# Query and key tiles woven between the SSM heads and the end of the convolution, and gates through tanh, in a two-layer hybrid encoder

## What is computed

```
xn  = RMSNorm(h)
u   = xn @ W_in
br  = [attention(u), conformer(u), ssd(u), fourier(u)]
h  += W_o( sum_b sigmoid(xn @ Wg_b + c_b) * br_b )
h  += FFN(RMSNorm(h))      # dense in layer 0, 8 experts top-2 in layer 1
h  += sigmoid(h @ Wpg) * (p[l] @ Wpp)
```

## Time and profile before

| | |
|---|---|
| median of 3 runs | 2463.49 us |
| lowest, highest | 2458.93, 2463.57 us |
| the profiled execution: time, span | 2454.93 us, 2453.2 us |
| mean granted clock of TensorE | 0.96 of full speed |
| PE busy, share of the span | 93% |
| DVE, ACT, POOL busy | 65%, 53%, 4% |
| layer 0 mixers, from the start to the norm ahead of the feed-forward | about 0 to 545 us |
| layer 1 mixers | about 787 to 1322 us |

### The profile page before, as it was taken

How to read it: one execution, slowest core, us unless ns; L and a number is a source line. 1 busy time by engine, 2 the same in 40 slices (tenths; PEclk the granted TensorE clock), 3 DMA queues, 4 the chain that set the end, 5 groups by cost and what they waited for, 6 DMA issues and landing times.

```text
span 2453.2 us, 38341 instructions
## 1 busy us (share of the span) xinstructions
PE 2290.8 (93%) x12832; PEld 2000.1 (82%) x12832; DVE 1601.3 (65%) x2481; ACT 1297.4 (53%) x1710; POOL 103.5 (4%) x120
## 2 busy tenths in 40 slices
PE   7979999979997997999997999999999999999997
PEld 6959788979996986878897787878787878788786
DVE  4974233655542795333454898989898989888882
ACT  4421345444432531145543776767676767777671
POOL 0041010000000022011000000000000000000000
PEclk9979999999999998999998999999999999999999
DMA  6413232525533431323332897979898989888881
GB/s 248 173 52 133 99 125 99 196 108 206 177 146 133 168 138 55 142 99 121 139 118 104 337 367 306 371 298 366 309 369 324 365 315 359 336 332 342 332 318 68
DMA packets 76073, 539.40 MB, mean 220 GB/s; under 512 B 8607, under 2 KB 8607, under 8 KB 11976
## 3 DMA queue, kind: packets, MB, share of 16 engines
q1 hardware_dynamic: 72188, 525.03, 56.5%
q0 software_dynamic: 3584, 12.58, 1.8%
q10 hardware_dynamic: 204, 0.54, 0.1%
HBM read 537.03 MB, written 1.10 MB: 219 GB/s over the span
## 4 chain that ended last, share of the span: by engine, by line
PE 84%; DVE 7%; issue 5%; ACT 3%; DMA 1%; DVEq 0%; ACTq 0%; SPq 0%
PE ps L491 22%; PE ps L742 19%; PE ps L744 18%; PE ps L743 18%; PE ps L686 2%; DVE cvfa L1440 2%; DVE wlo L1714 1%; PE ps L892 1%; PE ps L920 1%; ACT whi L1247 1%; PE ps L636 1%; PE ps L696 1%; PE ps L497 1%; DVE xn L1395 0%; DVE ring_lo L1403 0%
## 5 line engine op out<-in xcount | busy, mean ns | idle before, releaser
L1714 DVE TENSOR_TENSOR wlo<-ring,whi 128x1024 fp32r<-128x1024 f32 x746 | 874.5, 1222 | 149.3 <-ACT whi L1247 148.2
L1247 ACT ACTIVATE whi<-ring 128x1024 fp32r<-128x1024 f32 x746 | 749.4, 1054 | 117.8 <-PE ps L744 109.8
L744 PE MATMUL ps<-whi,xlo 128*128 128x512 f32 (+1 forms) x1160 | 428.7, 370 | 0.0
L742 PE MATMUL ps<-whi,xhi 128*128 128x512 f32 x904 | 374.9, 415 | 1.3 <-DVE wlo L1714 1.3
L743 PE MATMUL ps<-wlo,xhi 128*128 128x512 f32 x904 | 355.5, 393 | 0.0
L743 PE MATMUL ps<-xlo,whi 128*128 128x256 f32 x1024 | 292.5, 286 | 0.0
L491 PE MATMUL ps<-xn,ring 128*128 128x256 f32 x1280 | 286.9, 382 | 0.0
L491 PEld LDWEIGHTS ps<-xn,ring 128*128 128x128 f32 x1280 | 245.6, 193 | 33.9
L744 PEld LDWEIGHTS ps<-whi,xlo 128*128 128x128 f32 x1160 | 219.8, 190 | 39.0
L742 PE MATMUL ps<-xhi,whi 128*128 128x256 f32 x736 | 213.6, 290 | 24.0 <-DVE wlo L1714 9.8
L742 PE MATMUL ps<-whi,hhi 128*128 128x512 f32 (+1 forms) x576 | 213.4, 370 | 0.0
(11 more groups left out here) (237 smaller groups left out, 3421.9 us busy)
## 6 DMA issues: line engine op xcount, KB each, us to landing
ring<-w_experts SPq DMA_DIRECT2D x340, 1024.0 KB, 5.0
ring<-w_mixers SPq DMA_DIRECT2D x114, 1024.0 KB, 4.8
ring<-w_dense SPq DMA_DIRECT2D x33, 1024.0 KB, 4.8
ring<-w_ple SPq DMA_DIRECT2D x10, 1024.0 KB, 4.9
bias<-bias_rows POOLq DMA_DIRECT2D x16, 384.0 KB, 4.3
cvfa<-bias_rows POOLq DMA_DIRECT2D x16, 384.0 KB, 4.3
constants_sb<-constants SPq DMA_DIRECT2D x1, 1048.0 KB, 7.9
h<-x_in SPq DMA_DIRECT2D x1, 1024.0 KB, 5.5
```

What stands on the lines that cost most here:

```text
L742: pe.matmul(dst, lhs[0], rhs[0], start=first, stop=False, skip_group_check=True)
L744: return pe.matmul(dst, lhs[1], rhs[0], start=False, stop=last, skip_group_check=True)
L1247: act.activation(whi[:, slot, :], ring[:, j % RING, lo:lo + UNIT], ACT.Copy).then_inc(s_wh, 1)
L1714: dve.tensor_tensor(wlo[:, slot, :], ring[:, j % RING, lo:lo + UNIT], whi[:, slot, :], ALU.subtract).then_inc(s_wl, 1)
```

## The change

- TensorE: `conv_norm` and the old `ssm_heads` leave their places. After `ssm_prep`, `query_key_heads` runs the first heads' cumulative sums, and then, four times: five query or key tiles, the outputs of the two heads, the cumulative sums of the next two. The two sums of the LayerNorm come behind the third tile of the third and of the fourth step, into bank 3. Four tiles are left for the end. Loops are written out.
- VectorE: the last 28 convolution operations go into the first two head steps, 14 each, behind the mixing matrices; the centring goes into the third step and the scaling into the fourth. The zeroing of `mix` moves ahead of the convolution's part that stays. `head_y` waits for both heads' outputs, which share bank 2.
- ScalarE: exponentials, tile copies, root and SiLU in the matching order; the root for the SSM norm behind tile 20.
- `ssm_out`'s transposes go to banks 0 and 1 and no longer wait for the last tile copies; `attention` no longer waits at its start for ScalarE's copies of the SSM branch, but at its first transposes. GpSimd lays out pair i once tile 20 + i is copied and the last mixing matrix is made.
- Gates: sigmoid(x) is taken as (tanh(x/2) + 1)/2. ScalarE computes Tanh with scale 0.5 and half the bias (`half_b`, one small VectorE operation for each layer), VectorE adds 1 in the multiplication, and the factor 0.5 goes into `mix_out` and `ple`.

```diff
+CONV_LATE = CT * CONV_K - 28
...
-            def query_key(l, i, t):
+            def query_key(l, t):
...
+                if t < 2:
+                    pe.wait_ge(s_xtc, l * TT + (t + 1))
+                elif t < 4:
+                    pe.wait_ge(s_sc, l * 2 + (t - 1))
+                else:
+                    pe.wait_ge(s_pf, l * N_PROJ + (T_Q + t - 3))
...
-                chain(bank(7, second * SEQ, SEQ), [con("ones")] * CT, [cv[:, t, :] for t in range(CT)]).then_inc(s_lns, 1)
+                chain(bank(3, 0, SEQ), [con("ones")] * CT, [cv[:, t, :] for t in range(CT)]).then_inc(s_lns, 1)
...
+            def head_y(l, hh):
+
+                for g in range(SSM_GROUPS):
+                    pe.wait_ge(s_mm, l * SSM_HEADS + (2 * hh + g + 1))
...
+            def query_key_heads(l):
+
+                cumsums(l, 0)
+                for hh in range(SSM_HEADS // SSM_GROUPS):
+                    for t in range(5):
+                        query_key(l, 5 * hh + t)
+                        if hh >= 2 and t == 2:
+                            conv_norm(l, hh - 2)
+                    head_y(l, hh)
+                    if hh < SSM_HEADS // SSM_GROUPS - 1:
+                        cumsums(l, hh + 1)
+                for t in range(20, 24):
+                    query_key(l, t)
...
             def ssm_out(l):
                 pe.wait_ge(s_yc, l * SSM_YC + SSM_YC)
-                pe.wait_ge(s_pf, l * N_PROJ + N_PROJ)
...
+                    if u == 0:
+                        pe.wait_ge(s_ybs, l + 1)
...
-                    pe.wait_ge(s_ybs, l + 1)
+                    pe.wait_ge(s_pf, l * N_PROJ + N_PROJ)
...
-                conv_norm(l, 0)
-                conv_norm(l, 1)
                 ssm_prep(l)
-                ssm_heads(l)
+                query_key_heads(l)
                 ssm_out(l)
...
+                for hh in range(SSM_HEADS // SSM_GROUPS):
+                    decay(l, hh, 0)
+                    query_key(l, 5 * hh)
+                    decay(l, hh, 1)
+                    for t in range(1, 4):
+                        query_key(l, 5 * hh + t)
+                    if hh == 3:
+                        conv_root(l)
+                    query_key(l, 5 * hh + 4)
+                conv_silu(l)
+                query_key(l, 20)
                 act.wait_ge(s_yc, l * SSM_YC + 4)
                 act.activation(yst[:, 4:6], yst[:, 2:4], ACT.Sqrt).then_inc(s_ya, 1)
+                for t in range(21, 24):
+                    query_key(l, t)
...
-                act.activation(gs[:, m_ % 2, :], bank(first_bank + m_ % banks, SEQ, SEQ), ACT.Sigmoid,
-                               bias=pk[:, bass.ds(b * KT + (AT["b_gate"] + m_), 1)]).then_inc(s_sg, 1)
+                act.activation(gs[:, m_ % 2, :], bank(first_bank + m_ % banks, SEQ, SEQ), ACT.Tanh,
+                               bias=half_b[:, bass.ds(b * KT + m_, 1)], scale=0.5).then_inc(s_sg, 1)
...
                     head_mix(l, hh, n, 1)
+                    if hh < 2:
+                        conv(l, CONV_LATE + 14 * hh, CONV_LATE + 14 * hh + 14)
+                    elif hh == 2:
+                        conv_center(l)
+                    else:
+                        conv_scale(l)
                     for g in range(SSM_GROUPS):
                         head_y(l, hh, n, g)
...
-                dve.wait_ge(s_y, n + (g + 1))
+                dve.wait_ge(s_y, n + 2)
...
-                dve.tensor_tensor(gt[:, m_ % 2, :], gs[:, m_ % 2, :], bank(first_bank + m_ % banks, 0, SEQ), ALU.mult).then_inc(s_bt, 1)
+                dve.scalar_tensor_tensor(out=gt[:, m_ % 2, :], in0=gs[:, m_ % 2, :], scalar=1.0,
+                                         in1=bank(first_bank + m_ % banks, 0, SEQ), op0=ALU.add,
+                                         op1=ALU.mult).then_inc(s_bt, 1)
...
-                dve.memset(mix[:, :, :], 0.0).then_inc(s_mz, 1)
...
-                    dve.tensor_tensor(h[:, m_, :], h[:, m_, :], bank(m_ % 4, 0, SEQ), ALU.add).then_inc(s_hr, 1)
+                    dve.scalar_tensor_tensor(out=h[:, m_, :], in0=bank(m_ % 4, 0, SEQ), scalar=0.5, in1=h[:, m_, :],
+                                             op0=ALU.mult, op1=ALU.add).then_inc(s_hr, 1)
...
+                dve.tensor_scalar(half_b[:, :], par("b_gate", 0, N_BRANCHES * KT), 0.5, None, ALU.mult)
...
-                conv(l, 8 * EARLY_BLOCKS - 88, CT * CONV_K)
-                conv_norm(l)
+                dve.memset(mix[:, :, :], 0.0).then_inc(s_mz, 1)
+                conv(l, 8 * EARLY_BLOCKS - 88, CONV_LATE)
                 ssm_scores(l)
...
-                    pool.wait_ge(s_pf, l * N_PROJ + N_PROJ)
+                    pool.wait_ge(s_pf, l * N_PROJ + i + (T_Q + 21))
                     n = l * UNITS + i * 4
                     pool.wait_ge(s_s, n + 1)
-                    pool.wait_ge(s_yc, l * SSM_YC + 1)
+                    pool.wait_ge(s_mm, l * SSM_HEADS + SSM_HEADS)
```

More of the change, by code:

```diff
@@ L163, in trunk_program @@
         rms_t = sb("rms_t", [P, 2, SEQ])
+        half_b = sb("half_b_gate", [P, N_BRANCHES * KT])
         mixers = ExitStack()
@@ L622, in ssm_prep @@
                     m.then_inc(s_bc, 1)
[L624 to L647, removed]
@@ new lines, in cumsums @@
+            def cumsums(l, hh):
+                for g in range(SSM_GROUPS):
+                    pe.wait_ge(s_ua, l * SSM_HEADS + (2 * hh + g + 1))
+                    for part in range(4):
+                        m = pe.matmul(bank(g, part * P, P), con("ones"), ua[:, g, part, :], start=True, stop=True)
+                    m.then_inc(s_r, 1)
+            def head_y(l, hh):
+                for g in range(SSM_GROUPS):
+                    pe.wait_ge(s_mm, l * SSM_HEADS + (2 * hh + g + 1))
+                    for tt, parts in enumerate((((0, 0), (3, 0), (4, 1)), ((1, 0), (2, 1), (5, 1)))):
+                        lo = hh * 64 + g * 256
+                        m = chain(bank(2, g * P + tt * 64, 64), [mm_[:, g, b, :] for b, _ in parts],
+                                  [xs[:, s, lo:lo + 64] for _, s in parts])
+                    m.then_inc(s_y, 1)
@@ L1120, in ssm_heads @@
                     act.activation(xs[:, tt, :], bank(4 + tt), ACT.Copy).then_inc(s_xtc, 1)
[L1121 to L1136, removed]
+                for hh in range(SSM_HEADS // SSM_GROUPS):
[9 more added lines that the diff above has]
+                query_key(l, 20)
                 act.wait_ge(s_yc, l * SSM_YC + 4)
                 act.activation(yst[:, 4:6], yst[:, 2:4], ACT.Sqrt).then_inc(s_ya, 1)
+                for t in range(21, 24):
+                    query_key(l, t)
                 act.wait_ge(s_yt, l + 1)
                 for c in range(CT):
-                    m = act.activation(ybr[:, SSM * CT + c, :], bank(4 + c // 2, (c % 2) * SEQ, SEQ), ACT.Copy,
+                    m = act.activation(ybr[:, SSM * CT + c, :], bank(c // 2, (c % 2) * SEQ, SEQ), ACT.Copy,
                                        scale=par("ssm_norm", c))
@@ L1347, in ple @@
                         act.wait_ge(s_pt, l * KT + (m_ - 1))
-                    act.activation(gs[:, m_ % 2, :], bank(2 * (m_ % 2) + 1, 0, SEQ), ACT.Sigmoid).then_inc(s_pg, 1)
+                    act.activation(gs[:, m_ % 2, :], bank(2 * (m_ % 2) + 1, 0, SEQ), ACT.Tanh,
+                                   scale=0.5).then_inc(s_pg, 1)
             act.dma_start(relb_sb, relb).then_inc(s_relL, 16)
@@ L1533, in ssm_heads @@
             def ssm_heads(l):
-                with dve.Fori(0, SSM_HEADS // SSM_GROUPS) as hh:
-                    dve.wait_ge(s_sc, l * 2 + 2)
-                    dve.wait_ge(s_xtc, l * TT + TT)
+                dve.wait_ge(s_sc, l * 2 + 2)
+                dve.wait_ge(s_xtc, l * TT + TT)
+                for hh in range(SSM_HEADS // SSM_GROUPS):
                     n = l * SSM_HEADS + hh * 2
@@ L1875, in ple @@
                     dve.wait_ge(s_pg, l * KT + (m_ + 1))
-                    dve.tensor_tensor(mix[:, m_, :], gs[:, m_ % 2, :], bank(2 * (m_ % 2), 0, SEQ),
-                                      ALU.mult).then_inc(s_pt, 1)
+                    dve.scalar_tensor_tensor(out=mix[:, m_, :], in0=gs[:, m_ % 2, :], scalar=1.0,
+                                             in1=bank(2 * (m_ % 2), 0, SEQ), op0=ALU.add, op1=ALU.mult).then_inc(s_pt, 1)
                 dve.wait_ge(s_pt, l * KT + KT)
                 for m_ in range(KT):
-                    dve.tensor_tensor(h[:, m_, :], h[:, m_, :], mix[:, m_, :], ALU.add).then_inc(s_hr, 1)
+                    dve.scalar_tensor_tensor(out=h[:, m_, :], in0=mix[:, m_, :], scalar=0.5, in1=h[:, m_, :],
+                                             op0=ALU.mult, op1=ALU.add).then_inc(s_hr, 1)
             dve.sem_inc(s_bm, 2)
```

40 lines of the change are left out of this document (22 added, 18 removed).

## The result

The changed kernel takes 2379.04 us (median of 4 runs, 2371.9 to 2381.32) against 2461.21 for the kernel before (4 runs, 2457.08 to 2463.57): a ratio of 0.9663, 95% interval 0.9637 to 0.9689, so 82 us less, by the interval 77 to 89. Of the profiled executions the one after has a span of 2377.2 us against 2453.2, 76.0 less. Forecast were 76 us, and 2387 with a range from 2369 to 2407.

The account below looks back on a forecast made before the run. TensorE, holding 84% of the chain, was taken as the bound. Per layer 32.4 (reordering) + 5.8 (Tanh) - 0.2 (small edits) = 38.0 us saved, 76 in all: 2387 us against the median, range 2369 to 2407.

Parts of the forecast that it names:

- First term: From the end of TensorE's transposes to the query stage: a wait of 4.3 us a layer, ends 3.2 and 6.7.
- the two readings of the lock: GpSimd's `ua` held for VectorE's whole run of taps (4.3 us, chosen), or slipping in between two taps (3.2).
- Second term: Query stage: tiles, cumulative sums, head outputs and LayerNorm sums without gaps on TensorE, 102.5 us a layer.
- The cover: TensorE's work in each head step hides the other engines' chain; with fourteen taps VectorE is free 4.6 us early.
- Third term: Tail from the last query tile through transposes to the second scores: 8.0 us a layer, without a wait.
- The half clock behind the wait for `ua`: TensorE slowed after standing still about 1 us before `ua`: 1.5 us a layer charged, ends 0 and 3.0.
- Fourth term: Attention's gates: Tanh needs no table load beside Exp, saving 5.8 us a layer, ends 0 and 8.8.
- the loads stay: Rival at attention's gates: table loads remain with Tanh, so nothing is saved there; 2399 us, 8%.
- the stage runs at the lower clock: Rival in the query stage: clock stays at 0.50, tiles cost 83 us more a layer; 90 slower, 2553; 2%.
- the head chain outlasts its cover: Rival in the query stage: VectorE becomes the bound in a step, costing 16.7 us a layer; 2421 us, 9%.

Follow-up runs that it names:

- the second profile: Profile of the changed kernel run again, unedited: 2376.80 us, ratio 0.9661 to the kernel before.
- the taps ahead: The changed kernel with all 124 convolution operations ahead of the group scores again, none between the heads: 2400.44 us, ratio 0.9749 to the kernel before.

## Why the prediction was right, and where it was off

**First term, the wait ahead of the query stage: right.** Forecast were taps to 140.3 on the old scale and `ua` 2.76 behind. In the profile after the last tap ends at 145.76, `ua` at 148.52, again 2.76 behind. Tiles start at 149.56, 4.1 after the transposes against 4.3 (5.0 in the second profile, where the wait for `ua` was 1.8 us instead of 0.9). The choice between the two readings of the lock, which decided that term, is what the taps ahead show: one GpSimd operation held for the whole run of taps, and 12.56 us of TensorE's time with it. The Trainium skill (SBUF — State Buffer, Who interferes with whom) says that a VectorE instruction with two SBUF inputs contends with a GpSimd instruction that reads SBUF; that the pair is held "for the whole instruction" stands there beside VectorE's two-port modes, and I had read it for both. By a hold of one instruction that wait would not have been there. Both readings occur, though: where GpSimd's first operation came in the middle of a run of taps it was held to the run's end, in the kernel before, in the changed one and with the taps ahead; where it came two VectorE operations ahead of the taps, at 104.61, GpSimd took turns with them. What decides between the two no run here shows, so the forecast's choice was right for its place and no rule.

**Second term, the query stage: right.** 149.56 to 251.98 are 102.4 us against 102.5. The cover was even longer than computed: in step two VectorE stood idle for 6.6 us before its head outputs, not 4.6, since its chain to the mixing matrices took 9.6 us instead of 11.5; in the order before, each of ScalarE's exponentials stood behind a tile copy (copies at 193.92 and 197.36, exponentials at 194.20 and 197.64). In step four the scaled output came at 237.60, 22.95 behind the step's sums at 214.65 (forecast 22.9), against the outputs' end at 238.11. That 0.5 us of room held.

**Third term, the tail: right.** 251.98 to 259.81 are 7.8 us against 8.0.

**The half clock behind the wait for `ua`: oversized.** I charged 1.5 a layer. Neither profile of the changed kernel had half clock between transposes and second scores, with waits of 0.9 and of 1.8 us; behind the 12.56 us hole it came.

**Fourth term, Tanh: right in kind, undersized.** Forecast 5.8 a layer with an end at 8.8; 8.5 came. Tanh needed no load beside Exp, as the Trainium skill lists it (ScalarE: Activation LUTs, Table sets: the hidden batching unit), and the 64 loads became four. Both stretches of half clock that followed the holes went, while I had counted one: attention is 134.8 in every kernel with Tanh, whatever else was done. With Sigmoid it varies with the clock alone: 140.1, 141.7 and 143.3, with 3.4, 6.8 and 10.2 us at 0.50, costing half of that each; so the stalls themselves are 3.5 a layer (138.3 - 134.8), not the 2.8 that the waits add up to.

**What was not foreseen: the projections.** In the profiled execution they gave back 5.8 and 5.9. 3.4 of it is a stretch of 6.8 us at half clock which other executions, the kernel before with an unused tile among them, show in one layer, both or none; 1.7 is 3.4 us more at half clock at the layer's start, which also comes and goes. The rest, 0.7 to 0.8, goes with another cadence of the tiles, and that changes with `half_b`'s place; but how much the place costs was anything from 0.2 to 1.0 in the second layer, and in the first layer nothing came back when the tile was put last. I had costed the edit at 0.2 for its operation (it took 0.18) and had not thought of its 128 bytes.

**Luck.** That the two profiled executions lie 76.0 us apart, to a tenth the forecast, is luck. The stretches for which I had forecast 38.2 a layer (32.4 and 5.8) gave 42.7 to 42.8, 85.5 in all, and 9.5 went elsewhere: 11.8 back in the projections, 1.8 in the late branches, 4.0 gained in stretches that the change does not touch.

The medians are steadier: 34.2 and 33.4 a layer for the order in the two profiles, 8.5 for Tanh, 0.2 to 1.0 back, so 41 to 43 a layer and 82 to 85 in all, against 82 measured and 76 forecast. That takes it that half clock elsewhere averages out, which no run shows. The 6 us between forecast and measured gain are about the undersized fourth term (2.7 a layer) and the half clock charged for nothing (1.5), less what the projections took. The remaining 2 of the 8 between 2387 and 2379 are the kernel before, whose median was 2463.49 when I forecast and is 2461.21 with one more run.

Of the rivals, that the loads stay and that the stage runs at the lower clock are ruled out. That the head chain outlasts its cover did not happen, but can be made to: by the one execution with 60 taps in the first step it takes some 40 more taps in one step (an estimate: 60 less the 2.35 us of the wait, by 0.4 a tap, against 14), and it then bites first in ScalarE's queue of copies, not at the mixing matrices where I would have looked.

## What to carry to other kernels

Measure a hole from landmark to landmark, with its half clock and with the waits on its far side, and price its replacement as a gapless sequence of known pieces: here that sum, 114.8, lay within half a microsecond of both profiles, 114.4 and 115.2. When VectorE's work is pushed between other steps, look for who else is queued behind its long runs: the last engine to start (GpSimd here) can be what the busiest one waits for; here starting its work earlier, or cutting the run short, removed the wait. A gate whose function shares a table with its neighbours is worth more than the loads on the critical path, because small holes can pull the clock down behind them.

## What the runs showed of the hardware that was not expected

- A single 128x128 GpSimd operation that came in the middle of back-to-back VectorE operations with two SBUF inputs waited for the end of the run (21.67 us before, 23.9 of the 26.41 with all taps ahead), then the rest went at 0.39 each. Eight of them that started at 104.61, two VectorE operations ahead of a run of eight taps, took turns with the taps and were done in 5.54 us; the taps were 0.54 apart then instead of 0.397.
- Holes of 0.69 us at each pair's end were followed by half clock at one of four pairs of a layer (Sigmoid in the new order) or at two (both kernels in the old order); holes of 0.9 and 1.8 us in all ahead of the query stage were not, in either profile of the changed kernel.
- A stretch of 6.8 us at half clock came in some executions in the midst of the projections (83 to 90 in the profile after), where TensorE had no hole ahead of it: busy 6.00 of 6.00 us from 72 to 78 and from 78 to 84.
- With all mixer tiles moved by 128 bytes the projection tiles followed one another every 2.84 us and then every 2.81 or 2.88, instead of every 2.83; a layer's 130 us of projections became 0.2 to 1.0 us longer. Whether the bytes are all of it is not shown.
